# A two-block fp32 network on one core: constants moved into feed-forward stages, the start in quarters, three stage ends and the last stores in another order

## The chip, the cores and the metric

The kernel runs on one core of one Trainium2 chip. The metric is the device time of one launch in microseconds, the median over several executions. TensorE is written PE, VectorE DVE, ScalarE ACT, GpSimd POOL, SyncE SP.

## The reference

256 tokens of width 1024 pass through two blocks in fp32. The first has two layers; both run feed-forward (ffn), a mixer, feed-forward, and a gated projection of `p` (called ple here). The mixer of layer 0 is a recurrence, that of layer 1 a pooling.

```python
def first_block(...):
    h = x
    for i in range(2):
        h = h + 0.5 * swiglu(rms_norm(h, ffn1_norm[i]), ffn1_w_gate[i], ffn1_w_up[i], ffn1_w_down[i])
        hn = rms_norm(h, mix_norm[i])
        m = rglru_mixer(hn, ...) if i == 0 else pool_mixer(hn, ...)
        h = h + m
        h = h + 0.5 * swiglu(rms_norm(h, ffn2_norm[i]), ffn2_w_gate[i], ffn2_w_up[i], ffn2_w_down[i])
        gate = sigmoid(rms_norm(h, ple_norm[i]) @ ple_w_gate[i])
        h = h + gate * (p[i] @ ple_w_proj[i])
    return rms_norm(h, final_norm)
# rglru: conv of width 4, gates r, ig = sigmoid(...), a = exp(-8 * r * softplus(-a_param)),
#        h_t = a*h_{t-1} + sqrt(1-a^2)*ig*x_t, y = h*gelu(gate), y @ w_out
# pool:  trailing means over 2, 4, 8, 16 tokens minus the token, a 256x256 map per group of columns, bias, scale

def second_block(x, ...):
    for layer in range(2):
        h = rmsnorm(x, attn_norm[layer]);  proj = h @ w_in[layer]
        # differential attention (rope) and a two-way gated linear recurrence (lower bounds of its forget gate from lb_logits)
        x = x + (sigmoid(gate_a) * y_a + sigmoid(gate_b) * y_b) @ w_o[layer]
        h = rmsnorm(x, ffn_norm[layer])
        x = x + (silu(h @ w_gate[layer]) * (h @ w_up[layer])) @ w_down[layer]
    return rmsnorm(x, final_norm)
```

## The kernel before, in words

All weights stream from HBM once, as blocks of 1 MB (128 partitions x 2048 fp32). SP issues one load per block into `raw`, a ring of three. ACT copies the block to `hi` (fp32r, the rounded high part), DVE writes `lo` = `raw` - `hi`; both are rings of three. PE multiplies high and low parts in fp32r with the likewise split activations (`xT`, or `prod_hi` and `prod_lo`), three terms for each product. SP may load block n once `lo` of block n-3 is written; ACT may write `hi` of block n once PE has finished block n-3 (`block_used`). Every engine runs one hand-written program through the same list of stages (`plan`); `split_to(n)` in the ACT and DVE programs does the splits two blocks ahead of PE's block n.

The stages are norm+ffn (33 blocks, chunk by chunk: a gate block, an up block, a down block; the middle eight chunks in a hardware loop), the recurrent stage ("lru", 15 blocks), pool (1), ple (5) and mix (32). The stages of the six feed-forwards are numbered 0 to 5 below; 0 and 1 lie around the recurrence, 2 and 3 around the pooling, 4 and 5 in the second block.

Between two stages `h` (tokens by columns) is updated in four pieces, row half t and column half c. DVE updates a piece from PSUM, PE transposes it (`turns`), ACT and DVE write the high and low parts of `xT` (`piece`). `norm_rows` is the ACT side of this, `norm_pieces_of` the DVE side. After ple a piece takes a sigmoid on ACT (`gate`, line 706) and a product and a sum on DVE (`gated_rows`, lines 1400 and 1402). The root mean square is applied late: its statistics (ACT line 490, DVE lines 931 to 938) are taken beside the next stage's first products.

`constants` makes small tables. Before, ACT and DVE run part 0 (the recurrence's decay from `a_param`, 128 x 10, and the level masks) in the last chunk of ffn 0, part 1 (rope angles) before the last split of the first ple, part 2 (lower bounds) there in the second ple. Each part that needs a function of another table costs ACT a table load.

The start: SP loads `x` in two halves by rows, then three blocks. ACT issues the identity and the first gains. PE transposes pieces (0,0) and (1,0) of `h` as they land, and the third after DVE's marker `loaded` (line 1127), which stands in DVE's order behind its first `piece`. Both halves of block 0 are rounded by ACT (`split_first`, line 429). POOL first clears 7680 columns of `scr` (`band`), then issues 12 loads of gains, 12 of constants and 48 small ones of the recurrent gates' weights (`band_loaded`), all without a wait on the other engines.

The end (`rescale`): POOL multiplies `h` by the final gain into `xn` (line 341), DVE by the inverse root (line 1152), and SP stores the output in two halves of 512 KB.

## Time and profile before

| | us |
|---|---|
| median of 3 runs | 1779.27 (1776.74 to 1779.37) |
| the profiled execution | 1777.48 |
| its span, first to last instruction | 1775.7 |
| PE busy | 1741.5 (98%) |
| DVE busy | 1269.3 (71%) |
| ACT busy | 1005.5 (57%) |
| HBM read | 309.54 MB, 175 GB/s over the span |

The span is what the trace covers; the profiled execution's own time is 1.8 us longer. PE is busy in nearly all of it, so the time is PE's work plus the moments in which it waits. A PE row counts an instruction from its start to its modelled end, which overlaps the next one's start, so a group of matmuls is read from start to start. The granted clock is in parts of full speed: 1.00 is 2.4 GHz, 0.50 is 1.2 GHz.

### The profile page before, as it was taken

What the parts mean: (1) busy time and instruction counts of PE and PEld (TensorE: products, weight loads), DVE (VectorE), ACT (ScalarE), POOL (GpSimd) and SP (SyncE); (2) the same over time, 40 slices, a digit from 0 to 9 for tenths busy, and PEclk for the clock granted to TensorE, in tenths of its full rate; (3) what the DMA queues carried; (4) which work ended last, traced back from release to release, by engine and by line L of the source; (5) the groups of instructions that cost most, each with busy time, mean ns of one, the idle gap of its engine ahead of it and who ended that gap; (6) DMA issues with size and microseconds to landing.
All of it is one profiled execution on the core that took longest, in us unless ns stands there. A gap on an engine that the chain in (4) does not pass through costs nothing.

```text
span 1775.7 us, 25944 instructions
## 1 busy us (share of the span) xinstructions
PE 1741.5 (98%) x10360; PEld 1544.7 (87%) x10360; DVE 1269.3 (71%) x1604; ACT 1005.5 (57%) x1264; POOL 68.4 (4%) x99
## 2 busy tenths in 40 slices
PE   7999999999999999999999999999999999999998
PEld 6888898888878888888888999888888999988886
DVE  5766777766677666776667988867666998877665
ACT  6544657654467444654457766464446965555443
POOL 9100000000000000000001000000000000000001
PEclk9999999999999999999999999999999999999999
DMA  9755444665545665365545553356555453456552
GB/s 221 252 189 189 153 132 148 216 225 189 189 165 173 193 191 184 122 211 189 191 151 168 195 161 123 139 181 213 189 189 166 149 184 123 139 166 197 193 191 82
DMA packets 229683, 311.76 MB, mean 176 GB/s; under 512 B 6568, under 2 KB 203040, under 8 KB 229472
## 3 DMA queue, kind: packets, MB, share of 16 engines
q1 hardware_dynamic: 225600, 304.11, 52.7%
q0 software_dynamic: 3840, 6.44, 1.5%
q8 instruction: 57, 0.93, 0.2%
q14 instruction: 26, 0.21, 0.0%
q10 hardware_dynamic: 160, 0.07, 0.0%
HBM read 309.54 MB, written 1.05 MB: 175 GB/s over the span
## 4 chain that ended last, share of the span: by engine, by line
PE 85%; DVE 6%; ACT 5%; issue 2%; DMA 1%; ACTq 0%; DVEq 0%
PE psA L1747 26%; PE psD L1818 25%; PE psA L1752 14%; PE psA L1800 6%; PE psA L1701 3%; PE psA L1805 3%; DVE lo L870 2%; PE psA L1706 2%; PE psA L1818 2%; ACT hi L423 1%; PE psD L2075 1%; PE psA L1883 1%; DMA raw<-in_ffn_w_down 1%; PE psD L1883 1%; PE psD L2012 1%
## 5 line engine op out<-in xcount | busy, mean ns | idle before, releaser
L870 DVE TENSOR_TENSOR lo<-raw,hi 128x2048 fp32r<-128x2048 f32 x287 | 655.0, 2290 | 187.1 <-ACT hi L423 186.5
L423 ACT ACTIVATE hi<-raw 128x2048 fp32r<-128x2048 f32 x287 | 546.2, 1909 | 67.8 <-PE psD L1818 29.9
L1747 PE MATMUL psA<-xT,hi 128*128 128x512 f32 x2102 | 505.7, 391 | 2.6 <-ACT hi L423 1.5
L1747 PEld LDWEIGHTS psA<-xT,hi 128*128 128x128 f32 x2102 | 389.2, 189 | 81.7 <-DVE xT L897 3.5
L1752 PEld LDWEIGHTS psA<-xT,lo 128*128 128x128 f32 x2112 | 271.8, 191 | 11.3 <-DVE lo L884 0.3
L1752 PE MATMUL psA<-xT,lo 128*128 128x256 f32 x2112 | 276.3, 283 | 0.0
L1818 PE MATMUL psD<-hi,prod_hi 128*128 128x512 f32 x544 | 173.7, 393 | 4.0 <-DVE prod_lo L1227 4.0
L1818 PE MATMUL psD<-hi,prod_lo 128*128 128x512 f32 x544 | 172.0, 390 | 0.0
L1800 PE MATMUL psA<-hi,xT 128*128 128x256 f32 x1152 | 146.3, 285 | 0.0
L1800 PEld LDWEIGHTS psA<-hi,xT 128*128 128x128 f32 x1152 | 140.5, 192 | 2.6 <-issue 2.6
L1818 PE MATMUL psD<-lo,prod_hi 128*128 128x512 f32 x544 | 142.3, 389 | 0.0
L555 ACT ACTIVATE scr<-psA 128x512 f32<-128x512 f32 x66 | 39.4, 597 | 170.0 <-PE psA L1752 170.0
L570 ACT ACTIVATE prod_hi<-scr 128x512 fp32r<-128x512 f32 x66 | 41.7, 632 | 161.1 <-DVE scr L1225 161.1
L1818 PEld LDWEIGHTS psD<-hi,prod_lo 128*128 128x128 f32 x544 | 102.2, 188 | 21.9
L1818 PEld LDWEIGHTS psD<-lo,prod_hi 128*128 128x128 f32 x544 | 102.1, 188 | 21.3
L1818 PEld LDWEIGHTS psD<-hi,prod_hi 128*128 128x128 f32 x544 | 98.2, 189 | 21.5 <-DVE prod_lo L1227 2.6
L560 ACT ACTIVATE scr<-psA 128x512 f32<-128x512 f32 x66 | 39.3, 595 | 132.8 <-PE psA L1752 132.8
L1818 PE MATMUL psD<-hi,xT 128*128 128x512 f32 x368 | 101.2, 399 | 2.0 <-DVE xT L893 2.0
L1219 DVE TENSOR_TENSOR scr<-psA,scr 128x512 f32<-128x512 f32 x66 | 45.6, 691 | 75.1 <-ACT scr L560 74.9
L1208 DVE TENSOR_TENSOR scr<-psA,scr 128x512 f32<-128x512 f32 x66 | 45.5, 690 | 73.3 <-ACT scr L555 73.3
L1701 PE MATMUL psA<-xT,hi 128*128 128x256 f32 x704 | 90.6, 285 | 0.6 <-DVE xT L897 0.6
L1701 PEld LDWEIGHTS psA<-xT,hi 128*128 128x128 f32 x704 | 86.7, 192 | 1.3 <-DVE xT L897 1.2
(285 smaller groups left out, 1796.7 us busy)
## 6 DMA issues: line engine op xcount, KB each, us to landing
raw<-in_w_in SPq DMA_DIRECT2D x48, 1024.0 KB, 5.3
raw<-in_ffn_w_gate SPq DMA_DIRECT2D x44, 1024.0 KB, 5.3
raw<-in_ffn_w_up SPq DMA_DIRECT2D x44, 1024.0 KB, 5.3
raw<-in_ffn_w_down SPq DMA_DIRECT2D x44, 1024.0 KB, 5.1
raw<-in_w_gate SPq DMA_DIRECT2D x22, 1024.0 KB, 5.3
raw<-in_w_up SPq DMA_DIRECT2D x22, 1024.0 KB, 5.3
raw<-in_w_down SPq DMA_DIRECT2D x22, 1024.0 KB, 5.1
raw<-in_lru_w_in SPq DMA_DIRECT2D x10, 1024.0 KB, 5.1
```

Of the source, the lines that this page charges most:

```text
L423: act.activation(hi[:, n % RING, :], raw[:, n % RAW, :], ACT.Copy).then_inc(hi_ready, 1)
L555: act.activation(gate_l, psA[:, 0:2, S:2 * S], ACT.Copy).then_inc(gate_l_ready, 1)
L570: act.activation(span(prod_hi[:, c % 2]), prod[:, c % 2, :], ACT.Copy).then_inc(prod_hi_ready, 1)
L870: dve.tensor_tensor(lo[:, n % RING, :], raw[:, n % RAW, :], hi[:, n % RING, :].bitcast(F32), ALU.subtract).then_inc(lo_ready, 1)
L1208: dve.tensor_tensor(both(sil[:, c % 2, :]), psA[:, 0:2, 0:S], gate_l, ALU.add).then_inc(gate_summed, 1)
L1219: dve.tensor_tensor(up[:, c % 2], psA[:, 2:4, 0:S], up_l, ALU.add).then_inc(up_summed, 1)
L1701: pe.matmul(to[:, f * S:(f + 1) * S], w_hi[:, k, f * P:(f + 1) * P], x[:, k, :], start=(begin and f == 0 and k == 0 and x is xTh), stop=False)
L1747: pe.matmul(psA[:, bank + f, :], w_hi[:, k, f * P:(f + 1) * P], xT[:, k].rearrange("p e s -> p (e s)"), start=(k == 0), stop=False)
L1752: last = pe.matmul(psA[:, bank + f, 0:S], w_lo[:, k, f * P:(f + 1) * P], xTh[:, k, :], start=(begin and k == 0), stop=(k == KT - 1))
L1800: pe.matmul(to[:, t * FC:(t + 1) * FC], x[:, k, t * P:(t + 1) * P], w_hi[:, k, :], start=(t == 0 and k == 0 and x is xTh), stop=False)
L1805: last = pe.matmul(to[:, t * FC:(t + 1) * FC], xTh[:, k, t * P:(t + 1) * P], w_lo[:, k, :], start=False, stop=(t == 1 and k == KT - 1))
L1818: last = pe.matmul(to[:, 2 * t + c, :], x[:, k, ts], w[:, k, half_of[c]], start=(first and k == 0 and e == 0), stop=(final and k == 1 and ...
```

## The change

It has seven parts.

1. Start. `x` is loaded in four quarters, block 0 in two halves between them. PE runs nine matmuls on a tile of ones before the first transposes and six before the third, and waits for the landing of a quarter instead of DVE's marker. ACT loads its table before anything else. DVE rounds the first half of block 0 (`first_high`), ACT the second, after the third piece; both low halves stand ahead of DVE's fourth piece.
2. Blocks 3 and 4 of the run land in free columns of `scr` (`EARLY`), so SP issues them without a wait.
3. POOL's 48 loads of recurrent gate weights wait until the high parts of the run's first five blocks are written (`hi_ready` at 5). `a_param` is no longer one of POOL's constants: ACT's queue loads it as rows and PE transposes it after the first block of ffn 0.
4. `constants`: the exponential of the decay at ACT's head of ffn 0, the rest of it on DVE before the loop of ffn 0; rope angles on DVE before the loop of ffn 1, their sines at ACT's head of ffn 2; the lower bounds' sigmoid in the second ple's end, their exponential and logarithm inside the first mix beside others with the same table, their DVE part before the loop of ffn 4.
5. End of the recurrent stage: the last gate block is taken from PSUM before the scans, and the last three pieces stand ahead of a split.
6. Pool: DVE biases the three other pieces of `h` first and then writes all pieces of `xT`; the split of the next block moves behind the next norm's first two updates (`between`).
7. End of the run: DVE multiplies by the root and the gain in one instruction, POOL does nothing; piece (1,0) goes over ACT, which stores it from its own queue; SP stores a half of 512 KB and a quarter of 256 KB.

```diff
-                    if n_at >= RAW:
+                    if n_at == 0:
+                        return
+                    if n_at >= RAW + 2:
                         sp.wait_ge(lo_ready, n_at - RAW + 1)
...
             pool.wait_ge(band_zeroed, 1)
+            pool.wait_ge(hi_ready, RAW + 2)
             for m, w in enumerate((a["lru_w_a"][0], a["lru_w_x"][0])):
...
+            act.wait_ge(eps_ready, 2)
+            act.activation(col(SPARE), eps[:, 1:2], ACT.Copy)
...
                     split_to(n)
+                    if st["ffn"] in (0, 2):
+                        constants(st["ffn"] // 2)
                     act.activation(col(SPARE), eps[:, 1:2], ACT.Silu)
...
                         if i == 0:
                             norm_stats(late=True)
-                        if i == 2:
-                            constants(1 + stage[2])
                         n += 1
                     act.activation(col(SPARE), eps[:, 1:2], ACT.Sigmoid)
+                    if stage[2] == 1:
+                        constants(2)
...
+            def first_high():
+
+                cs = slice(0, BW // 2)
+                dve.wait_ge(first_landed, 16)
+                dve.tensor_copy(hi[:, 0, cs], raw[:, 0, cs]).then_inc(first_hi, 1)
...
+                    if st["ffn"] in (0, 1, 4):
+                        constants({0: 1, 1: 2, 4: 3}[st["ffn"]])
                     with dve.Fori(0, (CH - 3) // 2) as j:
...
-                            if st["ffn"] == 0:
-                                constants(0)
                             if nxt[0] == "pool":
                                 scale_pool()
...
-                    biased(1, 0)
-                    split_through(n + 1)
-                    piece(*pool_pieces[0], nth=st["gain"])
-                    biased(0, 1)
-                    piece(*pool_pieces[1], nth=st["gain"])
-                    biased(1, 1)
-                    for part in pool_pieces[2:]:
+                    for t, c in ((1, 0), (0, 1), (1, 1)):
+                        biased(t, c)
+                    split_through(n)
+                    for part in pool_pieces:
                         piece(*part, nth=st["gain"])
...
                     outputs(2, RT // 2)
-                    split_to(n)
                     for c in range(2, RT // 2):
                         piece(xc[:, 2 * c:2 * c + 2, :], (slice(2 * c, 2 * c + 2), slice(0, S)))
+                    split_to(n)
...
-                        return dve.tensor_scalar(h[:, t, half_of[c]], xn[:, t, half_of[c]], col(RSTD + t), None, ALU.mult)
+                        return dve.scalar_tensor_tensor(h[:, t, half_of[c]], h[:, t, half_of[c]], col(RSTD + t), gain[:, half_of[c]], ALU.mult, ALU.mult)
...
-                    pe.wait_ge(h_ready, ready + i + 1)
+                    if ready is None:
+                        pe.wait_ge(x_loaded[i], 16)
+                    else:
+                        pe.wait_ge(h_ready, ready + i + 1)
...
+            pe.wait_ge(dve_step, 1)
+            warm(9)
             pe.wait_ge(ident_loaded, 16)
...
+                    if st["ffn"] == 0:
+                        pe.wait_ge(cpos_exp, 1)
                     down(n + 5, n + 4, c0 + 1, 0, first=True)
```

PE at the start of the run, before (`ident,scr` is the transpose of the gains, `ident,h` of a piece of `x`):

```order
L1914 MATMUL psD<-ident,scr 128x8
L1883 MATMUL psA<-ident,h 128x128 x8
L1883 MATMUL psD<-ident,h 128x128 x4
L1747 MATMUL psA<-xT,hi 128x512 x4
L1883 MATMUL psA<-ident,h 128x128 x4
```

and now:

```order
L1970 MATMUL psD<-one_row 128x128 x9
L1965 MATMUL psD<-ident,scr 128x8
L1931 MATMUL psA<-ident,h 128x128 x8
L1970 MATMUL psD<-one_row 128x128 x6
L1931 MATMUL psD<-ident,h 128x128 x4
L1795 MATMUL psA<-xT,hi 128x512 x4
L1931 MATMUL psA<-ident,h 128x128 x4
```

Fifteen matmuls on ones were put in, and the order of the others is kept.

DVE at the end of the first ple, before: the last rows of the rope angles (14 rows of them stand ahead, and two splits before those), the last split, and the first update of `h`:

```order
L1099 SCALAR_TENSOR_TENSOR rope<-rope 128x16
L1102 TENSOR_SCALAR rope<-rope 128x16
L1104 TENSOR_SCALAR rope<-rope 128x16
L870 TENSOR_TENSOR lo<-raw,hi 128x2048
L1400 TENSOR_TENSOR scr<-scr,psA 128x512
L1402 TENSOR_TENSOR h<-h,scr 128x512
```

and now:

```order
L1031 MEMSET stat 128x1
L903 TENSOR_TENSOR lo<-raw,hi 128x2048 x3
L1451 TENSOR_TENSOR scr<-scr,psA 128x512
L1453 TENSOR_TENSOR h<-h,scr 128x512
L1451 TENSOR_TENSOR scr<-scr,psA 128x512
```

The three splits follow one another; the rope rows stand before the loop of ffn 1.

DVE in the pool stage, before:

```order
L1167 TENSOR_SCALAR scr<-scr,stat 128x4x128
L1172 TENSOR_TENSOR scr<-h,scr 128x512
L870 TENSOR_TENSOR lo<-raw,hi 128x2048
L897 SCALAR_TENSOR_TENSOR xT<-psA,gain_col,xT 128x256 x2
L1172 TENSOR_TENSOR scr<-h,scr 128x512
L897 SCALAR_TENSOR_TENSOR xT<-psA,gain_col,xT 128x256 x2
L1172 TENSOR_TENSOR scr<-h,scr 128x512
L897 SCALAR_TENSOR_TENSOR xT<-psA,gain_col,xT 128x256 x4
L1198 TENSOR_TENSOR h<-psD,scr 128x512 x2
```

and now:

```order
L1215 TENSOR_SCALAR scr<-scr,stat 128x4x128
L1220 TENSOR_TENSOR scr<-h,scr 128x512 x3
L936 SCALAR_TENSOR_TENSOR xT<-psA,gain_col,xT 128x256 x8
L1243 TENSOR_TENSOR h<-psD,scr 128x512 x2
L903 TENSOR_TENSOR lo<-raw,hi 128x2048
L936 SCALAR_TENSOR_TENSOR xT<-psA,gain_col,xT 128x128 x4
```

The split went from ahead of the pieces to behind two updates of `h`, and now stands ahead of the next norm's first piece.

## Rows read from the trace of the kernel before

**Rows 1.** The page's part 1: busy us (share of span) and instructions, whole span

```profile
PE 1741.5 (98%) x10360; PEld 1544.7 (87%) x10360; DVE 1269.3 (71%) x1604; ACT 1005.5 (57%) x1264; POOL 68.4 (4%) x99
```

**Rows 2.** Waits of PE, whole span: who for whom, us, times, longest

```profile
PE psA L1883 <- DVE h L1402: 4.9, 2, 2.6
```

**Rows 3.** Timeline of PE, 0 to 50 us: start, us, instruction, idle before and releaser

```profile
10.43 1.12 PE L1883 MATMUL psD<-ident,h 128*128 128x128 f32 x4 [2.99 <-DVE stat L1127]
11.45 2.07 PE L1747 MATMUL psA<-xT,hi 128*128 128x512 f32 x4
16.41 1.09 PE L1747 MATMUL psA<-xT,hi 128*128 128x512 f32 x4
32.71 3.91 PE L1747 MATMUL psA<-xT,hi 128*128 128x512 f32 x16 [1.51 <-ACT hi L423]
40.64 0.73 PE L1818 MATMUL psD<-hi,prod_hi 128*128 128x512 f32 x2 [2.11 <-DVE prod_lo L1227]
```

**Rows 4.** Timeline of ACT, 0 to 50 us

```profile
6.66 1.28 ACT L453 ACT_TABLE_LOAD   x1 [6.66 <-PE psA L1883]
30.66 1.91 ACT L423 ACTIVATE hi<-raw 128x2048 fp32r<-128x2048 f32 x1 [4.72 <-DMA raw<-in_ffn_w_up]
```

**Rows 5.** DMA issues, 17 to 34 us: KB each, us to landing

```profile
raw<-in_ffn_w_up SPq DMA_DIRECT2D x1, 1024.0 KB, 13.3
```

**Rows 6.** Timelines at the first ffn's end, DVE and PE

```profile
186.53 0.68 DVE L1056 CAST level_mask<-scr 128x1024 uint8<-128x1024 int32 x1
...
197.41 0.47 PE L1818 MATMUL psD<-hi,prod_hi 128*128 128x512 f32 x1 [1.84 <-DVE prod_lo L1227]
```

**Rows 7.** Timelines at the recurrent stage's end, DVE and PE

```profile
295.23 2.28 DVE L870 TENSOR_TENSOR lo<-raw,hi 128x2048 fp32r<-128x2048 f32 x1
...
298.17 3.92 PE L1818 MATMUL psD<-hi,xT 128*128 128x512 f32 x16 [0.90 <-DVE xT L893]
```

**Rows 8.** Timelines around the first ple's end: DVE, ACT, PE

```profile
525.75 2.29 DVE L870 TENSOR_TENSOR lo<-raw,hi 128x2048 fp32r<-128x2048 f32 x1 [2.19 <-ACT hi L423]
...
533.13 0.69 DVE L1400 TENSOR_TENSOR scr<-scr,psA 128x512 f32<-128x512 f32 x1 [0.70 <-ACT scr L706]
...
532.41 0.69 ACT L706 ACTIVATE scr<-psD,stat 128x512 f32<-128x512 f32 x1 [1.14 <-PE psD L1818]
...
529.43 0.66 PE L1883 MATMUL psA<-ident,h 128*128 128x128 f32 x4 [2.24 <-DVE h L1402]
...
535.08 1.20 PE L1752 MATMUL psA<-xT,lo 128*128 128x256 f32 x8
```

**Rows 9.** PE by stretch there: length, busy (instructions), granted clock, DMA share, GB/s

```profile
531.00:532.00 1.00, 1.00 (x4) 0.50 1.08 386
```

**Rows 10.** Timeline of PE at the second ple's end

```profile
949.03 0.65 PE L1883 MATMUL psA<-ident,h 128*128 128x128 f32 x4 [2.64 <-DVE h L1402]
```

**Rows 11.** Pool stage: timelines of DVE and PE, PE by stretch

```profile
723.10 2.29 DVE L870 TENSOR_TENSOR lo<-raw,hi 128x2048 fp32r<-128x2048 f32 x1
...
726.33 0.36 PE L1948 MATMUL psD<-hi,xT 128*128 128x256 f32 x1 [1.19 <-DVE xT L897]
...
728.00:730.00 2.00, 2.00 (x13) 0.58 1.01 358
```

**Rows 12.** Timeline of the last 10 us

```profile
1766.79 1.28 POOL L341 TENSOR_TENSOR scr<-h,gain 128x512 f32<-128x512 f32 x1
1766.95 1.14 DVE L938 SCALAR_TENSOR_TENSOR stat<-stat 128x1 f32<-128x1 f32 x1
1771.41 0.88 DVE L1152 TENSOR_SCALAR h<-scr,stat 128x512 f32<-128x512 f32 x2
```

**Rows 13.** Timelines at the head of a later ffn: ACT, DVE, PE

```profile
552.27 1.28 ACT L581 ACT_TABLE_LOAD   x1
...
556.90 0.69 DVE L1227 TENSOR_TENSOR prod_lo<-scr,prod_hi 128x512 fp32r<-128x512 f32 x1 [0.70 <-ACT prod_hi L570]
...
559.03 0.63 PE L1818 MATMUL psD<-hi,prod_hi 128*128 128x512 f32 x2
```

More of the change, by code:

```diff
@@ L58 @@
 PTOK = 8192
+EARLY = 8192, 10240
 L_R = 0
@@ L300, in _ @@
             assert n == TOTAL
-            updates = sum(s[0] in ("ffn", "lru", "pool", "ple", "mix", "renorm", "rescale") for s in plan)
-            for t in range(T):
-                sp.wait_ge(h_ready, 2 * T * updates + 2 * (t + 1))
-                sp.dma_start(out[0, t * P:(t + 1) * P, :], h[:, t, :]).then_inc(stored, 16)
-            sp.wait_ge(stored, 16 * T)
+            sp.wait_ge(row_scaled, 2)
+            sp.dma_start(out[0, 0:P, :], h[:, 0, :]).then_inc(stored, 16)
+            sp.wait_ge(row_scaled, 3)
+            sp.dma_start(out[0, P:2 * P, 512:D], h[:, 1, 512:D]).then_inc(stored, 16)
+            sp.wait_ge(stored, 16 * 3)
         @block.gpsimd
@@ L730, in soft @@
                         exponential(slice(d * HS, (d + 1) * HS))
+                        if not l and d:
+                            constants(3)
                         logarithm(slice(d * HS, (d + 1) * HS))
+                        if not l and d:
+                            constants(4)
                     def complement(d):
@@ L856, in _ @@
         def _(dve):
-            st = {"split": 0, "norm": 0, "updates": 0, "piece": 0, "ffn": 0, "step": 0, "rows": 0, "update": None, "early": 2, "gain": 0, "rescaled": 0, "updated": 0, "renorm": 0}
+            st = {"split": 0, "norm": 0, "updates": 0, "piece": 0, "ffn": 0, "step": 0, "rows": 0, "update": None, "early": 2, "gain": 0, "rescaled": 0, "updated": 0, "renorm": 0, "between": None}
             def step(ins):
@@ L1391, in _ @@
                             norm_stats(row=False)
-                        if i == 2:
-                            constants(1 + stage[2])
                         n += 1
@@ L1682, in _ @@
                     st["updates"] += 1
-            for c in range(2):
-                st["update"](1, c).then_inc(h_ready, 1)
         @block.tensor
```

144 lines of the change are left out of this document (94 added, 50 removed).

## The prediction

> **What bounds the kernel now.** The page's busy times come first: PE is busy for 1741.5 of 1775.7 us [rows 1], so all that can be won without less work is the 34 us in which it waits, and the time in which it runs at half clock. The waits of PE, longest first, say where: with two exceptions they are single events, not a toll on each block. The pair of waits for `h` [rows 2] is the end of the two ple stages. The timelines then give each place: in the start 2.99, 1.51 and 2.11 us [rows 3], at the end of ffn 0 1.84 [rows 6], at the end of the recurrence 0.90 [rows 7], in the ple stages 2.24 and 2.64 [rows 8, 10], in the pool 1.19 [rows 11]. The stretches show the second cost: behind the ple wait and behind the pool's the granted clock is 0.50 and 0.58 [rows 9, 11], which is the 1.2 GHz level. The reader should see that the change touches each of these places and nothing in the loops.
>
> The sum is made against the profiled execution, 1777.5 us. It lies 1.8 us under the median of the runs shown, 1779.3.
>
> **Start, 5.3 us.** Four matmuls at 11.45 take 2.07 us and four alike at 16.41 take 1.09 [rows 3]: the first ones run at half speed, though the stretch lists 1.00 as granted. Loading two quarters first brings both pieces that PE transposes first by about 5 us. The third no longer waits for DVE's marker, which was worth most of the 2.99 us. The table load of 1.28 us, which ACT did between PE's first transposes and its first piece [rows 4], is done during the transfers. DVE now has the chain: the rounding of half a block and then the pieces. I work out the first product for 9.4 us instead of 11.45 and, at full speed, block 0's end some 3.3 us earlier. If the fifteen new matmuls do not raise the clock, it is 2.3.
>
> Then block 3. It was issued once `lo` 0 was ready and took 13.3 us to land [rows 5], so ACT waited 4.72 for it [rows 4] and PE 1.51 [rows 3]. Landing in spare columns, it is there in time: 3.3 + 1.5 = 4.8 us. The next wait, 2.11 for `prod_lo`, came from the same lateness on ACT and DVE. Of it I count only 0.5: block 4 now shares the DMA engines with POOL's small constants, and ACT has a table load and an exponential more in front of the silu (1.28 + 0.2 us). The bounds: 6.9 if all three waits go, 2.5 if block 3 still lands late; I take 5.3, nearer the upper end, since 13.3 us of transfer begun at about 4 us still ends at 17, before ACT has time for it.
>
> **POOL's 48 gate loads** start at about 27 us instead of 24. They end in the fifties, and PE needs them after 260. Cost nothing by that cover. Behind them in POOL's order stands only the gain. They meet the loads of blocks 6 to 9; SP's queue isn't moved past them. Those have one block's time of PE more in hand than before, as DVE is no longer late; if the cover fails, it is a few us (second rival).
>
> **End of ffn 0, 1.8 us.** DVE did its constants from 186.53 on, and PE waited 1.84 for the last `prod_lo` [rows 6]. They leave this place. Where they go, DVE is late by about 5 us (mask 0.68, some twenty tiny ones) ahead of the loop. Queued behind them are the split of block 7 and chunk 2's gate sum; the split isn't wanted for some 8 us, so nothing is charged. The same holds for the rope rows before the loop of ffn 1 (3.7 us) and four rows in ffn 4. A stall here would be 0 to 2 us each.
>
> **End of the recurrence, 0.9 us.** The pieces stood behind a split of 2.28 us [rows 7] that isn't wanted for 5 us. They lead now, and the gelu gets its input 3 us earlier. The wait of 0.90 goes whole.
>
> **The two ple stages, 3.3 and 3.5 us.** DVE's last split began at 525.75 after waiting 2.19 for ACT, which stood waiting for the rope angles, and PE waited 2.24 behind it [rows 8]. Without the constants the split is over before PE finishes its share of the last block, so this wait goes and the half clock with it. But what is late next must be charged. From 527.2 (529.43 less 2.24) to the next stage's first product at 535.08 PE took 7.9 us. Its own work there is twelve 512-column matmuls at about 0.23 and three groups of transposes at about 0.36, so 3.8. The third group needs the gate (0.69), and on DVE, behind a piece, product and sum (0.69 each) [rows 8]. With PE on time these end at 531.4, 0.8 after PE. So 4.6 us remain of 7.9, a gain of 3.3. The second stage loses three table loads instead of one and had 2.64 [rows 10]: 3.5. Bounds: each 2.0 if the clock falls all the same, each 4.1 without any wait.
>
> **Pool, 1.6 us.** The split of 2.29 us ahead of the pieces [rows 11] goes behind two updates. PE starts the pool's products 0.7 us earlier, its second wait goes, and without the half clock it gains about 3. But DVE now splits just when PE wants the third piece of `h`, and PE then waits 1.6 us. I get 1.6, bounds -0.5 (the clock falls in that new wait) and 3.
>
> **The last stores, 1.2 us.** An operation on one column took 1.14 us on DVE while POOL multiplied, and ended with it [rows 12]; without POOL it takes the 0.2 of its neighbours. Against that DVE has one multiplication more (0.7). The last update of `h` and the last results then come 1.0 us earlier than the rows that begin at 1771.41 [rows 12]. Two quarters on two queues instead of a half give about 0.2. Bounds 0.3 and 2.
>
> **The head of ffn 2, nothing.** ACT gets a table load and two sines there, 1.6 us ahead of the silu. Before, `prod_lo` was ready at 557.6 and PE wanted it at 559.03 [rows 13]: 1.4 in hand, and 0.6 of ACT's time was waiting. It just fits, with 0.2 left; bounds 0 and 1.1, the latter if a switch took twice the 1.28 of its row. The instruction before this load is an ordinary one that ends where the load begins, so I count 1.28. The Trainium skill, in "ScalarE: Activation LUTs", "What ACT_TABLE_LOAD costs", adds a drain of about 1.38 us to each switch, 2.66 in all; with that the step would stall PE by 1.2 us, and the sum would be 16.4.
>
> Sum: 5.3 + 1.8 + 0.9 + 3.3 + 3.5 + 1.6 + 1.2 = 17.6 us. 1777.5 - 17.6 = 1759.9. The median before lies 1.8 above its profiled execution; I put the forecast a little towards it, 1760.5.
>
> **Rivals.**
> - *The waits move instead of going* (0.22). The ple and pool ends are bounded by the chain gate, product, sum, transposes, pieces, and PE's waits of 0.8 to 1.6 us there may still drop the clock: 1.3 less for each ple, 2.1 for the pool, 4.7 in all, 1765.2. For it: the pool's wait of 1.19 us was followed by 0.58 [rows 11]. Against it: 1.84 us in ffn 0 was followed by full clock.
> - *DMA stays the limit of the start* (0.12). Five blocks at once with POOL's small loads: block 4 late, later one of blocks 6 to 9 late behind the gate loads, as 13.3 us for one block shows is possible [rows 5]. The start gives 2.5 and one stall of 2 us comes back: 1765.3.
> - *A table switch costs ACT twice its row* (0.03): each of the two new switches ahead of a silu then stalls PE by 1.1 us, in ffn 2 and in ffn 0: 1762.7. Against it: the row begins with no gap [rows 13]. The Trainium skill's "What ACT_TABLE_LOAD costs" in "ScalarE: Activation LUTs" would have it about so, at 1762.9.
> - *The early matmuls do nothing for the clock* (0.06): the start gives 1.0 less, 1761.5.
> - *Slower than before* (0.02): DVE enters the loops of ffn 0 and ffn 1 5 and 3.7 us late, and doesn't catch up, because DVE, ACT and PE wait on each other in turn in each chunk. It decides from 1.1 us of wait for each of the 16 chunks on: 17.6 are then eaten. At 1.5 us, 24 come back and the time is 1784.5. Against it: DVE is idle for 29% of the time [rows 1].
>
> **How the numbers follow.** The forecast as worked out has 0.55, and its own bounds reach from 1756 to 1765. The first two rivals lie within 1768 with 3 us of spread; the range 1755.5 to 1767.5 leaves out two in ten at most. A measurement of this kernel tells 0.2%, 3.6 us, from no change. Only the last rival and a heap of misjudged places reach 1775.7: faster 0.95, same 0.03, slower 0.02.
>
> **What would show it.** In the changed profile: PE's waits in the start sum to under 3 us behind its first product, which starts near 9.4, and the first down block starts near 35; no wait at the end of ffn 0 or of the recurrence; waits of under 1 us at the ple ends with a granted clock of 1.00; one wait of about 1.6 us for the third piece behind the pool; no new wait in the loops of ffn 0 and 1; no POOL row at the end, and the one-column operation at 0.2 us. Wrong it is if half-clock stretches remain at ple or pool, or if PE waits for `hi` inside the first 80 us.

## The result, and the profile after

| | before | after |
|---|---|---|
| median of 4 executions, us | 1778.01 (1776.64 to 1779.37) | 1762.17 (1761.19 to 1763.34) |
| span of the profiled execution, us | 1775.7 | 1759.4 |
| PE busy, us | 1741.5 | 1738.7 |

The ratio is 0.9917, with a 95% interval of 0.9902 to 0.9932: 15.8 us less. The forecast was 1760.5, the range 1755.5 to 1767.5. The profiled execution of the changed kernel took 1761.2, 16.3 less than the profiled one before.

The page's part 1 of the changed kernel, against [rows 1]. POOL has lost its last multiplications; PE's share is now 99%:

```profile
PE 1738.7 (99%) x10391; PEld 1544.4 (88%) x10391; DVE 1268.5 (72%) x1608; ACT 1003.5 (57%) x1263; POOL 62.3 (4%) x94
```

The timeline of PE over the whole span, rows with an idle time before them (start, us, instruction, idle and releaser). These are the places of [rows 3, 6, 7, 8, 10, 11]:

```profile
10.50 1.19 PE L1795 MATMUL psA<-xT,hi 128*128 128x512 f32 x4 [1.55 <-DVE xT L936]
...
38.02 0.70 PE L1866 MATMUL psD<-hi,prod_hi 128*128 128x512 f32 x2 [3.02 <-issue]
...
203.23 1.22 PE L1749 MATMUL psA<-xT,hi 128*128 128x256 f32 x8 [0.20 <-DVE xT L936]
...
525.04 0.65 PE L1931 MATMUL psD<-ident,h 128*128 128x128 f32 x4 [0.49 <-DVE h L1453]
...
723.68 0.66 PE L1931 MATMUL psD<-ident,h 128*128 128x128 f32 x4 [0.89 <-DVE h L1243]
```

No wait stands at the end of ffn 0 or of the recurrence any more, the ple ends wait 0.49 each, the pool 0.89. One large wait is left, 3.02 us before the first down block (the first block of down weights, block 4 of the run), in the start.

The same points of both traces show where the 16.3 us of the span came from. The first is the start of the first down block, the others are the starts of the products that wait last for a piece of `xT` (the row with about 0.2 us of idle time at the head of each stage, such as the one at 203.23; "reference products" below):

| PE reaches | before | after | gained since the row above | predicted |
|---|---|---|---|---|
| first down block | 40.64 | 38.02 | 2.6 | 5.3 |
| recurrent stage | 208.05 | 203.23 | 2.2 | 1.8 |
| ffn 1 | 319.64 | 313.63 | 1.2 | 0.9 |
| ffn 2 | 538.97 | 529.20 | 3.8 | 3.3 |
| ffn 3 | 739.21 | 727.82 | 1.6 | 1.6 |
| second block | 958.58 | 943.35 | 3.8 | 3.5 |
| end of span | 1775.7 | 1759.4 | 1.1 | 1.2 |

Every term but one lies within 0.5 us. The start gave half of what was expected, 2.7 us too little, and the other six together gave 1.4 more than forecast (13.7 for 12.3): the nearness of the total is partly luck. ACT's timeline in the start shows what was late:

```profile
25.12 1.91 ACT L445 ACTIVATE hi<-scr 128x2048 fp32r<-128x2048 f32 x1
29.77 1.92 ACT L445 ACTIVATE hi<-scr 128x2048 fp32r<-128x2048 f32 x1 [2.74 <-DMA scr<-in_ffn_w_down]
31.71 1.28 ACT L540 ACT_TABLE_LOAD   x1
33.00 0.21 ACT L540 ACTIVATE cpos<-cpos 128x10 f32<-128x10 f32 x1
33.23 1.28 ACT L612 ACT_TABLE_LOAD   x1
```

Block 3 (25.12) was there in time. Block 4 was not: ACT waited 2.74 us for it, and behind its rounding stand two table loads and the exponential, then the silu and `prod_hi`, for which PE waits. The DMA issues of the first 34 us give the landing (KB, us to landing), against 13.3 for the late block of [rows 5]:

```profile
scr<-in_ffn_w_down SPq DMA_DIRECT2D x1, 1024.0 KB, 19.3
```

And the stretches of the core (busy us of PE, PEld, DVE, ACT, POOL, then granted clock, DMA share, GB/s) show that the DMA engines were full while few bytes moved. (The share sums the times of packets, which can overlap, so it can pass 1.) POOL's element-by-element constants (`conv_w`, `lru_c`, `lbt`) were in flight then:

```profile
20.00:24.00 4.00, 4.00 (x27) 3.64 (x26) 2.73 (x7) 3.89 (x12) 3.13 (x5) 1.00 1.10 186
24.00:28.00 4.00, 4.00 (x24) 3.48 (x24) 3.24 (x13) 3.00 (x5) 0.00 (x0) 1.00 1.20 96
```

### The profile page after: what moved, and what is told of

It reads as the page before. It is cut to its first block, busy times and chain, and to the rows that moved or that the text cites. A ratio compares the mean times of both kernels' runs of the same rounds, so it can differ in the third digit from the quotient of the medians.

```text
span 1759.4 us, 26008 instructions
## 1 busy us (share of the span) xinstructions
PE 1738.7 (99%) x10391; PEld 1544.4 (88%) x10391; DVE 1268.5 (72%) x1608; ACT 1003.5 (57%) x1263; POOL 62.3 (4%) x94
## 3 DMA queue, kind: packets, MB, share of 16 engines
HBM read 309.54 MB, written 1.05 MB: 177 GB/s over the span
## 4 chain that ended last, share of the span: by engine, by line
PE 91%; DVE 4%; ACT 3%; issue 1%; DMA 0%; SPq 0%; ACTq 0%; DVEq 0%
PE psD L1866 28%; PE psA L1795 27%; PE psA L1800 14%; PE psA L1848 6%; PE psA L1749 4%; PE psA L1853 3%; PE psA L1754 2%; PE psA L1866 2%; PE psD L2140 1%; DVE lo L903 1%; PE psD L2077 1%; PE psD L1931 1%; PE psA L1931 1%; DVE xT L936 1%; ACT hi L445 1%
```

## The experiments

The two theories for the missing 2.7 us are these. Theory A: block 4 lands late because POOL's constants share the DMA engines with it. Theory B: ACT's table loads and exponential ahead of the first silu. Line numbers of an experiment can differ by a few from those of the changed kernel. Each experiment is one execution with its trace, but for the two that were timed. Their spans are poor evidence for differences of 2 or 3 us: the kernel before, run beside them, took 1774.69, 1777.03 and 1776.71 us, against 1778.01 beside the change. What is read is the places in the traces.

Most places repeat within some tenths. The start doesn't: in the five traces that have the start of the changed kernel unedited (its own and those of the rope, pool order, decay and POOL experiments) the first down block begins at 38.02, 38.02, 37.75, 35.85 and 36.91. What repeats there is the chain. The first down block began 8.25 or 8.26 us behind ACT's rounding of block 4 in each of these, so its time follows block 4's landing. A difference in the start is therefore read from block 4's landing and from the length of this chain.

### POOL's constants held back

```diff
+            pool.wait_ge(hi_ready, RAW)
             for t_, src in ((level_words, a["c_level"]), ...
```

> The changed kernel, with POOL's eleven constants (c_level to lbt) issued only when the high parts of three blocks are written (about 19 us) instead of at 13.5. Theory A, landing: block 4 of the run is late because these loads, many of them element by element, share the DMA engines with it, and that makes PE's 3.0 us wait before the first down block. Then ACT rounds block 4 right behind block 3 at about 27.0 instead of 29.8, its 2.7 us wait is gone, prod_lo is ready near 34.6, PE's wait falls from 3.0 to under 0.5 and the first down block starts near 35.3 instead of 38.0; the span is shorter by 2.7. Theory B, ACT's tables: the wait comes from the exponential with its table load and the second table load ahead of the silu; then the first down block stays within 0.5 of 38.0. If block 4 is late because of the five large loads alone, ACT still waits over 2 us for it.

Span 1756.3, 3.1 us less than the changed kernel's. ACT now rounds blocks 3 and 4 in one go, the wait of 2.74 is gone, and so is PE's 3.02 (its first wait behind 14.43 is at 200.28). The stage after ffn 0 starts 2.95 us earlier (203.23 to 200.28). ACT and the core's stretches:

```profile
24.98 3.71 ACT L446 ACTIVATE hi<-scr 128x2048 fp32r<-128x2048 f32 x2
28.71 1.28 ACT L541 ACT_TABLE_LOAD   x1
```

```profile
28.00:32.00 4.00, 4.00 (x26) 3.53 (x25) 2.92 (x5) 3.94 (x6) 3.47 (x8) 1.00 0.85 21
```

The view of the DMA queues for 29 to 31 us has one row of traffic (packets, MB, share of the 16 engines), that of POOL's queue:

```profile
q0 software_dynamic: 129, 0.01, 92.3%
```

Block 4 lands 12.1 us after its issue instead of 19.3. This repeats where the first down block does not: in the seven traces that issue block 4 early with the constants beside it, it took 18.2 to 19.3 us, in the four with the constants held 12.1 or 12.2. From 29 to 31 us POOL's small loads run alone (the constants, and behind them the first of the gate loads, issued from 29.28 on) and take 92.3% of the DMA engines' time at 7 GB/s. Theory A holds, and the last sentence of the expectation is answered: the five large loads alone don't make block 4 late. The eleven loads were held together. One of them, `c_level`, has 512 KB, at the 368 GB/s of the changed kernel's stretch from 16 to 20 us some 1.4 us of transfer (an estimate) out of the 7.2 that block 4 gained; no run held it alone. The two table loads and the exponential were still there, and cost PE nothing in this execution.

### ACT's exponential moved

```diff
-                    if st["ffn"] in (0, 2):
-                        constants(st["ffn"] // 2)
+                    if st["ffn"] == 2:
+                        constants(1)
...
+                    if st["ffn"] == 0:
+                        constants(0)
+                        act.activation(col(SPARE), eps[:, 1:2], ACT.Silu)
```

> The changed kernel, with ACT's exponential of the decay moved from ahead of the first silu to behind the rounding of block 6, followed by a reload of the silu's table. Theory A: this takes 1.28 + 0.2 us out of ACT's chain behind block 4, so PE's wait of 3.0 falls to 1.5 and the first down block starts near 36.5; the landing of block 4 stays at 29.7. Theory B: the wait is the tables' and goes nearly whole, first down block near 35.1. If a table switch costs twice its row, 2.7 go. At the new place two table loads and the exponential (2.8 us) stand where ACT was idle for 1.6 us; up to 1.2 us may come back as a wait in the loop's first pass, else nothing.

Span 1757.7, PE's wait 1.36, first down block at 36.32. So 1.7 us, of which 0.2 is an earlier landing (block 4 rounded at 29.59 instead of 29.77) and 1.5 the load and the exponential (1.28 + 0.21). As theory A said. The chain confirms it, though 36.32 itself lies within the scatter of the start: from block 4's rounding to the first down block it is 6.73 us here and 8.25 in the unedited kernels. At the new place nothing came back: the stage after ffn 0 starts 1.67 us earlier, as much as the first down block (1.70). A and B both act in one chain, and either edit shortens it; only with the earlier landing did the wait go whole (in the first of two traces of that kernel; the second, below, has 0.91 left).

### Without the fifteen matmuls on ones

```diff
-            warm(9)
...
-                    warm(6)
```

> The changed kernel without the fifteen matmuls on ones. If they raise the clock of the first products: the first four 512-column matmuls take about 2.07 us as before the change instead of 1.19, block 0 ends 1.0 to 2.3 us later than 17.3, but the first down block stays at 38.0 within 0.3, because PE now waits 3.0 us there for ACT and DVE: in the changed kernel as it stands they are worth nothing at the end. If they do nothing for the clock: all rows of the start stay where they are. If the time of the run follows block 0's end, the span is 1 to 2 us longer.

PE's timeline without them:

```profile
11.01 2.07 PE L1795 MATMUL psA<-xT,hi 128*128 128x512 f32 x4 [1.15 <-DVE xT L936]
...
37.92 0.70 PE L1866 MATMUL psD<-hi,prod_hi 128*128 128x512 f32 x2 [0.42 <-issue]
```

Four products take 2.07 us instead of 1.19, so the early matmuls do raise PE's clock. In nine of the ten traces with them the four take 1.16 to 1.21 us, in the four without them (two are of the kernel before) 2.04 to 2.07; the tenth is in the experiment on the pool's order. The first down block starts at 37.92 all the same, and the wait ahead of it is 0.42 instead of 3.02: what they won was waited away there. The span of 1759.8 is 0.4 above the changed kernel's. That arose at the head of ffn 1, far from the edit: ACT waited 2.53 us for a down block's landing there, and PE 0.27 at 334.04. The other trace without these matmuls and the second one of the kernel before have such a wait in ffn 1 too (0.37 and 0.45), the rest have none.

### Blocks 3 and 4 issued later

```diff
-                    if n_at >= RAW + 2:
+                    if n_at >= RAW:
```

> The changed kernel, with blocks 3 and 4 landing in the same spare columns, but issued only when the low parts of blocks 0 and 1 are written, as before the change (about 13.7 and 18.1 us). Theory A, landing: block 3 lands near 27 and block 4 later than 31.7, both stand behind POOL's constants; PE waits for block 3 (up to 1.5 us) and the first down block starts at 40 to 43. Theory B: tables bound the first down block, it starts less than 1 us later than 38.0.

```profile
9.92 1.20 PE L1795 MATMUL psA<-xT,hi 128*128 128x512 f32 x4 [1.53 <-DVE xT L936]
...
38.48 0.81 PE L1866 MATMUL psD<-hi,prod_hi 128*128 128x512 f32 x2 [3.99 <-issue]
39.09 1.05 PE L1866 MATMUL psD<-hi,prod_lo 128*128 128x512 f32 x2
```

Neither theory's number. Block 3 was not late at all, and the first down block came only 0.5 us later: block 4 was rounded 0.5 later (30.23), and the chain behind it took the same 8.25. The first product was 0.6 earlier (9.92), but that isn't shown to come of the edit: it came at 9.92 in the experiment on POOL too, where the start was left as it was. So issuing early is close to worthless while the constants are in the way; my expectation of 40 to 43 took the landings of the kernel before for granted. Block 3, issued at 13.20, landed in 8.1 us, and block 4, issued at 17.09, in 13.1. The span, 1761.4, is 2.0 longer all the same: behind the wait of 3.99 the down block ran at half clock for a while (pairs at 1.05 us instead of 0.62), which cost 1.6.

### The rope angles back in the first ple

```diff
-                    if st["ffn"] in (0, 1, 4):
-                        constants({0: 1, 1: 2, 4: 3}[st["ffn"]])
+                    if st["ffn"] in (0, 4):
+                        constants({0: 1, 4: 3}[st["ffn"]])
...
+                        if i == 2 and stage[2] == 0:
+                            constants(2)
```

(and the two sines on ACT likewise)

> The changed kernel, with the rope angles back in the first ple (DVE's rows ahead of the last splits, ACT's two sines there); the second ple is left as changed, as a control in the same run. Theory A, split late and clock with it: DVE's split waits about 2.2 us again, PE waits about 2.2 before the last gated products, the granted clock falls to 0.5 behind it, and ffn 2's first product comes 3.8 us later against the end of ffn 1's loop; nothing changes in the second ple (4.2 us from PE's wait for h to the next stage's first product, waits 0.49 and 0.19). Theory B, only the wait counts and the clock would fall anyway or not at all: 2.2 us later. Third, the rows' new place before the loop of ffn 1 had a price of its own: then the stretch of ffn 1 (313.6 to 525.0) is shorter than 211.4 by some tenths.

```profile
38.02 1.19 PE L1870 MATMUL psD<-hi,prod_hi 128*128 128x512 f32 x2 [3.18 <-issue]
...
525.88 0.66 PE L1935 MATMUL psA<-ident,h 128*128 128x128 f32 x4 [2.26 <-DVE h L1457]
...
534.42 1.20 PE L1799 MATMUL psA<-xT,hi 128*128 128x512 f32 x4 [0.21 <-DVE xT L938]
```

The wait of 2.26 is back, but the clock did not fall behind it. From ffn 1's reference product (316.45) to ffn 2's (534.42) it took 217.97, against 215.57 in the changed kernel and 219.33 before. So of the 3.8 us at this place 2.4 are the wait and its order, and 1.4 were the half clock of [rows 9]. The second ple took its 4.2 us as in the changed kernel. The third possibility, a price of the rows' new place, does not show: from ffn 1's reference product to the end of PE's work ahead of the ple's transposes it is 207.2 us here and 207.1 in the changed kernel.

The same execution lost 2.8 us in the start, where nothing was edited. PE waited 3.18 us there, as in the changed kernel (3.02), but this time its clock was down when it went on:

```profile
38.00:40.00 2.00, 1.98 (x5) 1.61 (x6) 2.00 (x1) 1.00 (x1) 2.00 (x5) 0.50 0.17 33
```

The same wait, at the same place of the same code, is followed by full clock in one execution and by half clock in another.

### The old order in the pool stage

```diff
-                    for t, c in ((1, 0), (0, 1), (1, 1)):
-                        biased(t, c)
-                    split_through(n)
-                    for part in pool_pieces:
+                    biased(1, 0)
+                    split_through(n + 1)
+                    piece(*pool_pieces[0], nth=st["gain"])
...
```

> The changed kernel, with the old order in the pool stage on DVE (split of the next block ahead of the pieces, bias and pieces in turn). Theory A, as in the prediction: a wait of 1.2 us is back ahead of the pool's products' end, the granted clock falls below 0.7 behind it, the 0.89 wait for the third piece goes, and the next ffn's first product comes 1.6 us later than at 727.8. Theory B, the clock falls with any wait near 1 us: then the clock also fell in the changed kernel, and the difference is under 0.8.

The wait of 1.19 came back and the clock stayed at 1.00 (before: 0.58 [rows 11]):

```profile
716.25 0.36 PE L2011 MATMUL psD<-hi,xT 128*128 128x256 f32 x1 [1.19 <-DVE xT L936]
...
718.00:720.00 2.00, 1.95 (x17) 1.75 (x15) 2.00 (x6) 0.59 (x1) 0.00 (x0) 1.00 0.90 313
```

The stage (709.59 to 728.17) took 18.58, against 17.93 in the changed kernel and 19.55 before. The order of instructions is worth 0.65 and the clock was worth 1.0; the 1.6 of the prediction was the sum of the two. Neither theory had this: the wait came without the clock.

In the start of this execution, which was not edited, the clock fell in spite of the fifteen matmuls on ones:

```profile
10.67 1.68 PE L1798 MATMUL psA<-xT,hi 128*128 128x512 f32 x4 [1.60 <-DVE xT L936]
...
12.00:14.00 2.00, 2.00 (x8) 1.65 (x7) 2.00 (x6) 1.18 (x5) 2.00 (x5) 0.50 1.11 344
```

Nearly the same idle time, 1.52 to 1.59 us, was followed by full clock in six other traces. Block 1's products came at 18.66 instead of 17.48, and the wait before the first down block absorbed it (1.54 instead of 3.02). So the fifteen matmuls make full clock at the first product likely, not certain.

### The decay back in the last chunk of ffn 0

```diff
-                    if st["ffn"] in (0, 1, 4):
+                    if st["ffn"] in (1, 4):
...
+                            if st["ffn"] == 0:
+                                constants(1)
```

> The changed kernel, with DVE's part of the decay and the level masks back in the last chunk of ffn 0; ACT's exponential stays at the head. Theory A: PE waits 1.8 us again for the last prod_lo of ffn 0 and the recurrent stage's first product comes 2.0 to 2.2 us later than at 203.2. Rival: the 2.2 us that the change gained between the first down block and the end of ffn 0 came partly from elsewhere (the head, block 5 and 6 of the run); then it is 1.8 or less later and 0.4 shows between 38 and 60 us.

A miss. PE waits 0.22 for the last `prod_lo` instead of 1.84:

```profile
190.95 0.47 PE L1868 MATMUL psD<-hi,prod_hi 128*128 128x512 f32 x1 [0.22 <-DVE prod_lo L1272]
```

From the first down block (35.85) to the recurrent stage (201.61) it took 165.76, against 165.21 in the changed kernel and 167.41 before. DVE's rows at that place are worth 0.55 us. This kernel has the same DVE rows there as the one before, but not ACT's exponential with its table load. The trace of the kernel before shows what that cost: DVE, having made the input, stood idle for 1.74 us until ACT had loaded the table and done the exponential.

```profile
189.04 0.17 DVE L1061 TENSOR_SCALAR cpos<-cpos 128x10 f32<-128x10 f32 x1 [1.74 <-ACT cpos L518]
```

That is close to the 1.62 by which PE's wait is shorter here (0.22 for 1.84). So most of the 2.2 us belong to this chain; no kernel had the exponential alone there. The span was 1757.7, 1.7 under the changed kernel's, for a reason apart from the edit, as far as the trace tells: block 4 was issued at 9.38 instead of 10.45, landed in 18.2 us instead of 19.3, and was rounded at 27.60 instead of 29.77.

### POOL busy in the last 10 us

```diff
+                if kind == "rescale":
+                    for i in range(3):
...
+                        pool.tensor_tensor(xn[:, i // 2, ...], gain[:, cs], gain[:, cs], ALU.mult)
```

> The changed kernel, with three multiplications of 128 x 512 on POOL in the last 10 us whose result nobody reads (the work that the change took away, with other data). Theory A, POOL's work holds up DVE's small operations: one of the one-column operations on DVE takes about 1.1 us instead of 0.16 and ends with a POOL row, and the span grows by 0.5 to 1.2 us. Theory B, the old row of 1.14 us was a wait for data: all one-column rows stay at 0.14 to 0.22 and the span stays within 0.3.

```profile
1751.95 0.89 DVE L979 SCALAR_TENSOR_TENSOR stat<-stat 128x1 f32<-128x1 f32 x1
...
1749.78 3.04 POOL L369 TENSOR_TENSOR scr<-gain 128x512 f32<-128x512 f32 x3 [585.01 <-DVE h L1337]
```

The kernel before had four such multiplications, here are three. The operation on one column took 0.89 us instead of 0.22 and ended at 1752.84, with POOL's last (1752.82). It had been so before: 1766.95 + 1.14 and 1766.79 + 1.28 both give 1768.1 [rows 12]. From the start of PE's last matmul to the end it is 8.1 us instead of 7.4. So DVE is held up by POOL's work itself, not by data. The rows beside POOL's work that read one tensor (0.21 at 1751.43 and 0.16 at 1751.75) or that came when POOL was done were not. The Trainium skill, in "SBUF — State Buffer", section "SBUF: two separate sides", describes a port pair over which a DVE operation with two SBUF inputs and a POOL operation that reads SBUF exclude each other, the one that starts first for its whole instruction; these rows agree with it.

### Three edits, and the first of them alone, timed

The three are the constants held, the exponential moved, and:

```diff
                 if early:
                     take_gains(0)
-                    first_high()
                 piece(*parts[0], nth=st["gain"])
                 update(0, 1).then_inc(h_ready, 1)
                 piece(*parts[1], nth=st["gain"])
                 if early:
+                    first_high()
                     early(0)
```

> The changed kernel with three edits: POOL's constants held until three blocks are rounded, ACT's exponential behind the rounding of block 6, and DVE's rounding of block 0's first half moved behind its first two pieces. The third edit alone should bring the first product from 10.5 to 9.4 or 9.6 us, since DVE stood idle for 2 us before that rounding, waiting for the load, while its pieces only needed ACT. With the other two nothing then holds PE at the first down block, which should start at 34.0 instead of 38.0 (35.0 with the first edit alone). Span 1755.3, median about 1757.5, against 1756.3 and 1758.1 for the first edit alone. Rival: the chain of the first down block ends again behind PE (then it starts near 35.0, and the second and third edits are worth nothing).

> The changed kernel with POOL's constants held, timed: 1758.5, that is 3.0 to 3.5 us below the changed kernel's 1762.2 and 0.5 to 1.5 above the kernel with all three edits. If the single look at it was a lucky execution, it comes out at 1760 or more.

| | median, us | executions | ratio to before (95%) |
|---|---|---|---|
| three edits | 1758.37 | 1757.82 to 1759.00 | 0.9898 (0.9882 to 0.9915) |
| constants held alone | 1758.81 | 1758.58 to 1759.14 | 0.9900 (0.9883 to 0.9916) |
| the change (timed apart) | 1762.17 | 1761.19 to 1763.34 | 0.9917 (0.9902 to 0.9932) |

Both were timed against the kernel before at 1776.71 on the same chip, the change at another time against 1778.01. By their medians they lie 3.4 to 3.8 us under the change; by the distance to the kernel before beside each (17.9 and 18.3, against 15.8) it is 2.1 and 2.5. Their slowest execution is 2 us faster than the fastest of the change. The intervals of the ratios overlap, since the kernel before scatters by 5 us between chips and executions, so the times alone do not show the gain; the traces place it. The two can't be told from each other by time. In PE's timeline of the three edits there is no wait between 14.23 and 199.95; the first down block starts at 34.79. In the trace of the one edit this time a wait of 0.91 is left there (down block at 35.69): ACT began block 3 at 25.65 instead of 24.98, and the two table loads and the exponential stand in the chain behind it. So the second edit can take out what the first one leaves, 0.9 us here. For the three edits 34.0 was expected; 34.79 is near the rival's 35.0, but with PE never waiting.

The third edit was a misreading of mine:

```profile
7.45 1.40 DVE L940 SCALAR_TENSOR_TENSOR xT<-psA,gain_col,xT 128x128 fp32r<-128x128 f32 x5 [1.71 <-ACT xT L476]
...
10.37 1.16 PE L1799 MATMUL psA<-xT,hi 128*128 128x512 f32 x4 [1.22 <-DVE hi L928]
```

DVE's pieces waited for ACT until 7.45, only 0.8 us earlier than they had started behind the rounding. What then stands on DVE ahead of the first product, eight piece instructions and the rounding, is 2.8 us in any order. The product came at 10.37 instead of 10.50.

### Three edits without the matmuls on ones

> The kernel with three edits, without the fifteen matmuls on ones. In the changed kernel their removal was hidden by PE's wait before the first down block. With that wait gone it should show: first products at half clock (about 2.07 us for four), block 0 ends 1.5 to 2.3 later, and the first down block starts at 35.5 to 36.3 instead of 34.0, the span is as much longer. If another limit has taken over, under 0.5.

```profile
10.82 2.04 PE L1799 MATMUL psA<-xT,hi 128*128 128x512 f32 x4 [0.98 <-DVE hi L928]
...
37.05 0.63 PE L1870 MATMUL psD<-hi,prod_hi 128*128 128x512 f32 x2
```

The first down block comes at 37.05 instead of 34.79: 2.3 us. Block 1's products were as much later (19.68 for 17.39). The same fifteen matmuls that were worth nothing with the wait in place are worth 2.3 us without it. (The span is 3.0 longer; the other 0.7 arose later, most of it at the head of ffn 1, where PE waited 0.37 at 333.20.)

### The kernel before, once more

> The kernel before, once more, for its waits and its clock. Waits are set by the program and should stand within 0.1 us where they stood: 2.24 and 2.64 at the ends of the two ple stages, 1.84 at the end of ffn 0, 0.90 at the recurrence's, 1.19 in the pool. Theory A, the clock follows the waits by rule: half-clock stretches stand behind both ple waits and the pool's again. Theory B, whether a wait of 1 to 3 us is followed by the lower clock differs from execution to execution (in the changed kernel with the rope angles put back, a wait of 2.26 was followed by full clock): then at least one of these three places runs at 1.00 and the span differs from 1775.7 by 1 to 2 us for each.

The waits stand where they stood: 2.24 and 2.70 at the ple ends, 1.84, 0.89 and 1.18 at ffn 0, the recurrence and the pool. The clock does not. Stretches at the first ple, the pool and the second ple:

```profile
533.00:534.00 1.00, 1.00 (x5) 0.80 (x4) 1.00 (x4) 0.30 (x1) 0.00 (x0) 0.50 1.04 371
...
728.00:730.00 2.00, 1.64 (x11) 1.45 (x12) 2.00 (x5) 2.00 (x3) 0.00 (x0) 1.00 0.78 242
...
950.00:952.00 2.00, 2.00 (x11) 1.46 (x11) 1.97 (x4) 1.14 (x5) 1.38 (x2) 1.00 1.01 331
```

Half clock behind the first wait again, full clock behind the other two. The pool stage took 18.58 (19.55 in the first trace), the part from ffn 3 to the second block 218.43 (219.37). In the start, where the first trace had full clock behind a wait of 2.11, it fell in this one behind 2.08:

```profile
42.00:44.00 2.00, 2.00 (x6) 1.52 (x6) 1.12 (x2) 0.84 (x2) 2.00 (x5) 0.50 0.47 42
```

That cost 1.6 us (40.37 to 198.72 against 40.64 to 197.41), and the span came out at 1775.5, nearly the same by another route. Theory B holds: a wait makes the lower clock possible, and whether it comes differs between executions. The Trainium skill says of a kernel's start, in "TensorE: Matmul & The Clock Gate", part 1, that the number of slow matmuls differs from run to run. These two traces agree: the second group of four 512-column products took 1.59 us in the first (at 14.03) and 1.17 in this one (at 13.79).

Not tried: POOL's 48 gate loads without their wait, `c_level` held alone, the old order at the recurrence's end, the constants back in the second ple, the last stores' two queues, and the late issue of blocks 3 and 4 together with the constants held.

## Why the prediction was right where it was, and where it was not

**What bounds the kernel** held: PE's single waits and the half clock behind them were the stock, and they paid nearly in full, 16.3 of some 17.6 us. Of the 16.3, 3.3 are the half clock that the first trace of the kernel before happened to have at three places (1.4, 1.0 and 0.9); its second trace had it at the first of them and in the start. That the forecast counted all three and met this very trace is luck, and so is it that the start's missing 2.7 us were half made up elsewhere. Of the signs named, the absent waits, the full clock at ple and pool, the last 10 us and the loops came as written; the first product (10.50 for 9.4), PE's waits behind it (3.35 in sum for under 3), the first down block (38.02 for 35) and the third piece's wait (0.89 for 1.6) did not.

**The start is the mis-sized term: 2.6 us for 5.3.** Four steps of it failed.
- "The first product for 9.4", for which the prediction shows no sum, was 10.50. DVE waited for the half block until 7.67 [1.92 of idle], and the 2.8 us of DVE's work follow. With the rounding put last DVE still began at 7.45, so the half block was not the only limit. The quarters landed at 3.46 and 4.88, but PE's first transposes began at 5.48, as before (5.47): in the traces where PE stood idle ahead of them it waited for the identity's load. What came earlier is ACT's first piece (6.26 for 7.95), mostly by the table load of 1.28 that no longer stands ahead of it.
- "Block 0's end some 3.3 us earlier" was therefore some 2, and block 3 started 3.5 us earlier instead of 4.8. That block 3 would be there in time was right; the experiment on the issue shows that the early issue was not what did it.
- "Transfer begun at about 4 us" did not begin then. SP's issuing of the loads took time itself: block 3's stands at 7.09 and block 4's at 10.45, each over 3 us long. Block 3 took 14.4 us and not 13.3.

```profile
10.45 3.46 SPq L280 DMA_DIRECT2D scr<-in_ffn_w_down  x1
```

- "Of it I count only 0.5", for the wait of 2.11, was on the right wait with the wrong sign: it grew to 3.02. I named POOL's small constants as sharing the engines and then charged them nothing in microseconds. The row of 13.3 us for a block in flight beside them [rows 5] was a bound I read as an argument for "still ends at 17". Block 4 took 19.3. The rival "DMA stays the limit of the start" described this with 2.5 for the start, and it was 2.6; its second half, a stall among blocks 6 to 9 behind the gate loads, did not come, so the total lay between it and the forecast. The gate loads themselves began at 32.28 and not at 27, as they wait for block 4, and ended in time all the same.

**The end of ffn 0**, 2.2 for 1.8, right in size and wrong in its reason: DVE's own rows account for 0.55, and DVE's wait of 1.74 for ACT's exponential for most of the rest. "Nothing is charged" for DVE's lateness into the loops held in both ffns.

**The end of the recurrence**, 1.2 for 0.9: the group behind the wait took 3.92 us [rows 7] and takes 3.79 without one, 0.13 of the 0.3 that the place gave beyond its wait; the rest is open. The order was not put back in a run, so that it is the order that did it is argued from the wait being gone.

**The ple ends.** "4.6 us remain of 7.9" was 4.73 (the transposes at 520.72 to the product at 525.45). The rest of the 3.8 is 0.1 behind it and 0.5 in ffn 1 and the ple's own blocks, where no cause was sought. The 3.5 for the second stage follows from no sum shown: by that of the first, with 2.64 for 2.24, it would be 3.7; it gave 3.8. But "this wait goes and the half clock with it" counts as certain what the kernel before has only in some executions: 1.4 of 3.8 at the first, 0.9 at the second ple.

**The pool**, 1.6 for 1.6, by a wrong path: the third piece waits 0.89 and not 1.6, the order gives 0.65, the clock gave 1.0.

**The last stores**, 1.3 for 1.2: from the end of PE's last matmul (1767.42 before, 1752.42 after) to the end of the span it was 8.3 us and is 7.0. The one-column row took 0.16.

**ffn 2's head** held: no wait. The prediction's "0.2 left" is a slip, 1.4 and 0.6 less 1.6 leave 0.4, and so much it is: `prod_lo` ended at 548.82, and PE took it up at 549.26. The 16.4 that stands beside it is too low by as much. A table switch costs its row: 1.28 us of load between neighbours that touch it, and taking one out with its exponential gave 1.5. The Trainium skill's 2.66 for a switch ("ScalarE: Activation LUTs", "What ACT_TABLE_LOAD costs") is not seen here, and that rival is out. So is the one that the early matmuls do nothing for the clock (2.07 against 1.19), though in the change as it stands they are worth nothing at the first down block. The rival of moved waits is out in its form, as all waits of 0.5 to 0.9 us at ple and pool kept full clock in every trace; the large wait that moved is the one in the start.

## What to carry to other kernels

A load of a few kilobytes that goes element by element can occupy the DMA engines for as long as megabytes do (block 4 came 7 us later for eleven loads of 0.6 MB in all, most of it in one): price it by the DMA share of the stretch, not by its size, and keep it away from the first big loads. An improvement ahead of a wait is worth nothing until that wait is gone, so test each part again once the last wait of its chain falls. And price a wait without its half clock; take what a single trace shows of half clock behind it as luck that can go either way. An edit ahead of the first big loads needs more than one trace, since they land up to 2 us apart from one execution to the next.

## What the runs showed of the hardware

- POOL's small loads alone held 92.3% of the DMA engines' time at 7 GB/s, from 29 to 31 us of the kernel with the constants held. Beside them a block of 1 MB took 18.2 to 19.3 us to land, and 12.1 or 12.2 when they came later.
- At the first down block of ffn 0 PE's waits of 2.08, 2.48, 3.18 and 3.99 us were followed by half clock (pairs of 512-column matmuls at 1.05 us, for 3 to 6 us), and those of 3.02, 2.11, 1.54, 1.36 and 1.07 by full clock. At the pool one of 1.19 was followed by half clock in one trace and by full clock in two, and in the start one of 1.60 by half clock where 1.59 kept it full. The length of the wait doesn't decide it. Behind the waits under 1 us at the ple ends, pool and later stages the traces of the changed kernel showed none.
- A DVE operation with two SBUF inputs on one column took 0.89 to 1.14 us beside POOL's multiplication, and ended within 0.02 us of it; those with one input beside the same work took 0.16 and 0.21.
